# Other weights for prompt attention in the background clock of a one-core decoder step

## The chip, the cores and the metric

One core of one Trainium2 chip runs the whole program in one launch. The metric is the device time of an execution in microseconds (us). The kernel before takes 4103.84 us, the median of three runs (4091.96 to 4107.23). The profiled execution took 4089.54 us, and its trace spans 4087.7 us.

## What is computed

One layer of a decoder for a prompt of 1024 tokens and 64 sample tokens (8 sequences of 8), all in float32. Cut to what matters here:

```
h  = rmsnorm(x) * (1 + scale1) + shift1
z  = h @ w_in                                   # q, k, v, conv inputs, two gates
B  = dilated window attention, 3 head groups, (window, dilation) = (128,1), (512,4), (2048,16)
A  = gated short convolution of z
x += gate1 * ((sigmoid(ga) * (B @ w_attn_o) + sigmoid(gc) * (A @ w_conv_o)) @ w_o)
h  = rmsnorm(x) * (1 + scale2) + shift2
q  = h @ w_query;  scores against 2 x 128 sub-keys; per token and head the best 16 of 16384 experts
x += gate2 * sum over 8 heads x 16 experts of softmax(score) * gelu(h . expert_u[e]) * expert_v[e]
y  = rmsnorm(x)
```

The retrieval reads, for every token, head and choice, one row of `expert_u` and one of `expert_v` (4 KB each).

## The kernel before

The 1088 tokens are nine tiles of up to 128 rows: tiles 0 to 7 are the prompt, tile 8 the sample. The kernel is one function, `peer`, with a program per engine and semaphores between them. Two kinds of work run side by side.

**Jobs.** A job is one head of one tile, 72 in all, of 16 *expert rows* (8 in tile 8). An expert row is the k-th choice of all 128 tokens: GpSimd (POOL) gathers 128 rows of `expert_u` into a ring of 9 slots (L863) and 128 rows of `expert_v` into a ring of 8 (L873), alternately; VectorE (DVE) takes the dot products (L2033); then the weighted sum over `expert_v` is made either by TensorE (PE; `weigh`, L1251, two matmuls of 512 columns by a diagonal matrix) or by DVE (L2049). In jobs 0 to 55 each takes every other row. A gather into a ring slot waits until the row that was there has been used, so POOL waits for PE's `weigh` and for DVE.

**The background.** The dense work is cut in four segments of tiles, (0), (1, 2), (3, 4, 5), (6, 7, 8). For each, `chain_order` lists items in a fixed order: the projection to q, k, v (`qkv`, L1036), the convolution's projections (`conv`, L1143), prompt attention (`s`, `t`, `o`, `oturn`), in the last segment the sample's attention (`kt`, `ss`, `pt`, `so`, `st`), `mix` (L1164), `out` (L1193), and the queries and scores of the jobs (`project`, `turn_q`, `score`, L1220 to L1237). Segment 0 runs ahead of the jobs; the dense work of segment g + 1 runs among the jobs of segment g. Each item goes PE, then ScalarE (ACT) or DVE, through one of four PSUM banks in turn; SyncE (SP) loads weight blocks into a ring of three slots as the items that read the old block finish.

In prompt attention an item is one head of one tile. `s` fills one bank with the scores of up to four blocks of 128 keys (a mask matmul L1074 and a score matmul L1075), DVE takes the row maximum (L1832, L1838), ACT the exponential (L1492), PE transposes the probabilities (`t`, L1111), ACT copies them (L1511), PE multiplies by the values (`o`, L1098) and ACT scales the result (L1521). The scores of the next item are issued before the outputs of this one.

**The clock.** PE, ACT and DVE each run their own list of background items, and after each piece of a job they advance it with `pace.up_to(limit(s, f))`: job s, fraction f done. DVE does so after every expert row, PE after every row that it weighs (three of its own rows ahead), ACT twice a job. `limit` works by the running sum `spent` of `chain_cost` over the items, between *marks* at jobs 0, 5, 21, 45 and 51: between two marks the items that are due are those whose share of the cost is not over the share of expert rows done. So `chain_cost` decides only how the rows between two marks are spread over the items between the same marks:

```
goal = spent[na] + (spent[nb] - spent[na]) * (now - clock(a)) / (clock(b) - clock(a))
due = max(i for i, c in enumerate(spent) if c <= goal)
return min(last_bg, max(na, due, number["score", item_of(min(s + 3, JOBS - 1))]))
```

The stretches between the marks hold 80, 256, 384 and 96 expert rows. Stretch 1 (jobs 0 to 4) holds the dense work of tiles 1 and 2, stretch 2 (jobs 5 to 20) that of tiles 3 to 5, stretch 3 (jobs 21 to 44) that of tiles 6 to 8, stretch 4 queries alone. From job 51 on there is no background. An item of a prompt tile t reads t + 1 blocks of the widest group, up to five of the second and up to two of the first, four blocks to a bank. So the attention of stretch 1 is 8 items with 16 banks of `s` and 16 of `t`, that of stretch 2 12 items with 40 and 40, that of stretch 3 8 items with 32 and 32; and one `oturn` for two items.

Of the kernel before, what the change touches and what calls it, by code (L numbers as in the profile page):

```python
# [237 lines left out]
def cols(g):  # L238
    return prompts(g) * P + (size(g) - prompts(g)) * NS
# [118 lines left out]
def chain_cost(key):  # L358
    name = key[0]
    if name == "conv":  # L360
        return 8 * max(240, cols(key[1])) / 600
    if name == "mix":
        return KC[key[3]] * max(240, cols(key[1])) / 600
    if name == "out":
        a, b = OUT_COLS[key[3]]
        return 8 * (b - a) / 600
    return {"project": 3.4, "qkv": 5.1, "s": 1.2, "o": 1.5, "t": 0.6, "kt": 0.6, "ss": 3.2, "so": 7.5}.get(name, 0.5)


def weight_blocks():  # L370
# [70 lines left out]
def peer(nc, io):  # L441
    with ExitStack() as ctx:
# [120 lines left out]
        for key in number:  # L563
            cost += chain_cost(key)
            spent.append(cost)
# [1624 lines left out]
```

## Time and profile before

| | us |
|---|---|
| median of three runs | 4103.84 |
| profiled execution | 4089.54 |
| its span | 4087.7 |
| PE busy | 3203.6 |
| DVE busy | 2904.9 |
| POOL busy | 2238.6 |
| ACT busy | 671.2 |

The DMA engines moved 1458.83 MB, a mean of 357 GB/s; 1142.49 MB of it by the queue of the expert gathers. The page of the profile cuts the span in 40 equal slices; the view by windows gives the busy time of each engine, the granted TensorE clock (1.00 is 2.4 GHz, 0.50 is 1.2 GHz; a value between is a mean of both), the mean busy share of the 16 DMA engines and what they moved, for any stretch of time. The DMA share counts the time that packets take, and can be a little over 1. The boundaries of the windows below are the starts of the first matmul of each part of the background on PE.

### The profile page before, as it was taken

Reading aid. Unit: us, or ns where it says so; the run is one execution under the profiler, and the core shown is the slowest. Engines: PE = TensorE matmul, PEld = TensorE weight load, DVE = VectorE, ACT = ScalarE, POOL = GpSimd, SP = SyncE. Lnnn points to the kernel's source line nnn. Section 1 sums busy time; section 2 is a strip of 40 time slices with the busy share of each in tenths; the row PEclk is TensorE's granted clock in tenths of the full one; section 3 lists DMA queues with packets and bytes.
Section 4 is the critical chain, followed back from the end, with each engine's and each line's share of the span. In section 5 each row is a group of like instructions: output and inputs, shape, how many; then the busy total and the mean of one; then the engine's idle time right before and its main releaser. Section 6 shows DMA issues by size and latency. Waiting matters only on the chain.

```text
span 4087.7 us, 35782 instructions
## 1 busy us (share of the span) xinstructions
PE 3203.6 (78%) x10406; PEld 1817.5 (44%) x10406; DVE 2904.9 (71%) x6586; ACT 671.2 (16%) x1872; POOL 2238.6 (55%) x2189
## 2 busy tenths in 40 slices
PE   5987989888889998887888977677877765566566
PEld 2575757654445544554444543334544431122222
DVE  1215645678876687677887777767778888888887
ACT  0012021221012211222101331111111110010111
POOL 0003323555554566565665566545657677777765
PEclk8988979999997899998998888788988877788878
DMA  6989969999997899999999899999999999999998
GB/s 207 274 268 334 316 219 315 368 404 383 389 364 244 289 385 398 377 394 382 391 394 366 307 359 366 359 365 363 400 355 406 407 407 409 409 399 409 409 368 319
DMA packets 670924, 1458.83 MB, mean 357 GB/s; under 512 B 53745, under 2 KB 378737, under 8 KB 670705
## 3 DMA queue, kind: packets, MB, share of 16 engines
q0 software_dynamic: 313648, 1142.49, 72.4%
q1 hardware_dynamic: 316596, 267.84, 21.0%
q10 hardware_dynamic: 40488, 46.22, 3.3%
q8 instruction: 87, 1.43, 0.1%
q14 instruction: 105, 0.86, 0.1%
HBM read 1422.53 MB, written 33.83 MB: 356 GB/s over the span
## 4 chain that ended last, share of the span: by engine, by line
DMA 17%; DVE 9%; POOL 9%; PE 8%; issue 5%; SPq 3%; ACT 1%; ACTq 0%; DVEq 0%; POOLq 0%
DMA peer_vring<-in_expert_v,peer_idx 12%; POOL peer_uring L863 4%; POOL peer_vring L873 4%; PE peer_psA L1251 4%; DVE peer_uring L2033 3%; DMA peer_uring<-in_expert_u,peer_idx 2%; DVE peer_acc L2049 2%; SPq L715 2%; SPq L711 1%; DMA peer_w<-in_w_in 1%; DMA peer_w<-in_w_attn_o 1%; PE peer_psB L1075 1%; PE peer_psB L1098 1%; PE peer_psB L1143 1%; DMA peer_arena<-in_x_prompt 1%
## 5 line engine op out<-in xcount | busy, mean ns | idle before, releaser
L1251 PE MATMUL peer_psA<-peer_vring,peer_diag 128*128 128x512 f32 x2336 | 1321.4, 704 | 527.2 <-DMA peer_vring<-in_expert_v,peer_idx 345.9
L873 POOL DMA_INDIRECT peer_vring<-in_expert_v,peer_idx x1088 | 1115.9, 1026 | 1129.2 <-PE peer_psA L1251 837.1
L2033 DVE CUSTOM_DVE_ANT_0 peer_uring<-peer_uring,peer_psH 128x1024 f32<-128x1024 f32 x1088 | 1320.8, 1214 | 327.3 <-DMA peer_uring<-in_expert_u,peer_idx 322.5
L863 POOL DMA_INDIRECT peer_uring<-in_expert_u,peer_idx x1088 | 1117.0, 1027 | 498.9 <-issue 299.2
L1251 PEld LDWEIGHTS peer_psA<-peer_vring,peer_diag 128*128 128x128 f32 x2336 | 485.6, 222 | 1184.5 <-issue 999.5
L2049 DVE SCALAR_TENSOR_TENSOR peer_acc<-peer_vring,peer_coef,peer_acc 128x1024 f32<-128x1024 f32 x495 | 637.1, 1287 | 89.8 <-DMA peer_vring<-in_expert_v,peer_idx 84.3
L1143 PE MATMUL peer_psB<-peer_hT,peer_w 128*128 128x128 f32 (+3 forms) x1152 | 277.0, 399 | 32.7 <-DMA peer_w<-in_w_in 32.5
L1220 PE MATMUL peer_psB<-peer_w,peer_hT 128*128 128x256 f32 x1152 | 275.8, 395 | 30.0 <-DMA peer_w<-in_w_query 29.3
L1036 PE MATMUL peer_psB<-peer_w,peer_hT 128*128 128x384 f32 (+1 forms) x864 | 294.9, 496 | 1.4 <-issue 0.7
L1164 PE MATMUL peer_psB<-peer_hT,peer_w 128*128 128x128 f32 (+3 forms) x1024 | 257.8, 407 | 35.0 <-DMA peer_w<-in_w_attn_o 35.0
L1220 PEld LDWEIGHTS peer_psB<-peer_w,peer_hT 128*128 128x128 f32 x1152 | 229.2, 201 | 89.3 <-DMA peer_w<-in_w_query 31.5
L1143 PEld LDWEIGHTS peer_psB<-peer_hT,peer_w 128*128 128x128 f32 x1152 | 199.2, 193 | 116.7 <-DMA peer_w<-in_w_in 36.3
L1164 PEld LDWEIGHTS peer_psB<-peer_hT,peer_w 128*128 128x128 f32 x1024 | 182.7, 198 | 111.6 <-DMA peer_w<-in_w_attn_o 39.5
L1036 PEld LDWEIGHTS peer_psB<-peer_w,peer_hT 128*128 128x128 f32 (+1 forms) x864 | 161.8, 190 | 131.3 <-issue 44.1
L1698 ACT ACTIVATE peer_g<-peer_g 128x16 f32<-128x16 f32 (+1 forms) x72 | 15.5, 215 | 1139.5 <-DVE peer_g L2063 1138.0
L1649 ACT ACTIVATE peer_diag<-peer_ident,peer_coef 128x128 f32<-128x128 f32 x584 | 178.3, 387 | 54.9 <-DVE peer_coef L2073 54.9
L1832 DVE TENSOR_REDUCE peer_mx<-peer_psB 128x1 f32<-128x512 f32 (+2 forms) x92 | 56.1, 626 | 124.0 <-PE peer_psB L1075 123.4
L1193 PE MATMUL peer_psB<-peer_w,peer_mT 128*128 128x384 f32 (+3 forms) x432 | 130.3, 458 | 6.3 <-issue 4.5
L1075 PE MATMUL peer_psB<-peer_w,peer_mT 64*128 64x256 f32 (+3 forms) x272 | 121.6, 532 | 0.0
L1098 PE MATMUL peer_psB<-peer_w,peer_arena 128*128 128x64 f32 x648 | 102.0, 317 | 24.2 <-ACT peer_arena L1511 24.0
L1098 PEld LDWEIGHTS peer_psB<-peer_w,peer_arena 128*128 128x128 f32 x648 | 99.1, 235 | 35.9 <-issue 35.9
L1193 PEld LDWEIGHTS peer_psB<-peer_w,peer_mT 128*128 128x128 f32 (+1 forms) x432 | 80.8, 188 | 59.0 <-issue 19.7
(201 smaller groups left out, 2738.0 us busy)
## 6 DMA issues: line engine op xcount, KB each, us to landing
peer_w<-in_w_in SPq DMA_DIRECT2D x136, 512.0 KB, 9.0
peer_w<-in_w_in SPq DMA_DIRECT2D x24, 1536.0 KB, 17.1
peer_w<-in_w_query SPq DMA_DIRECT2D x32, 1024.0 KB, 17.0
peer_w<-in_w_ada SPq DMA_DIRECT2D x16, 1536.0 KB, 8.0
peer_uring<-in_expert_u,peer_idx POOLq DMA_INDIRECT x1088, 11.4
peer_vring<-in_expert_v,peer_idx POOLq DMA_INDIRECT x1088, 11.2
peer_w<-in_w_conv_o SPq DMA_DIRECT2D x32, 384.0 KB, 10.0
peer_w<-in_w_o SPq DMA_DIRECT2D x8, 1536.0 KB, 22.2
```

What stands on the lines that cost most here:

```text
L863: pool.indirect_dma_start(out=uring[:, r % U, :], out_offset=None, in_=io["expert_u"], in_offset=bass.IndirectOffsetOnAxis(ap=idx[:, s % 4 ...
L873: pool.indirect_dma_start(out=vring[:, r % V, :], out_offset=None, in_=io["expert_v"], in_offset=bass.IndirectOffsetOnAxis(ap=idx[:, s % 4 ...
L1036: last = pe.matmul(dst[0:R, 0:WQKV], hT[:, k, i * P:i * P + R], wv[:, k, :], start=(k == 0), stop=(k == DC - 1))
L1098: last = pe.matmul(bank(key_o)[:, 0:HD], pT[:, t_slot[g, it, b] % 2, (at % 4) * P:(at % 4 + 1) * P], vv[:, kb, col:col + HD], start=(at == ...
L1143: last = pe.matmul(dst[:, 0:m], wv[:, k, part, :], hT[:, k, 0:m], start=(k == 0), stop=(k == DC - 1))
L1164: last = pe.matmul(dst[:, 0:m], wv[:, KC_AT[q] + k, :], src[:, k, 0:m], start=(k == 0), stop=(k == KC[q] - 1))
L1193: last = pe.matmul(dst[0:R, 0:e - a], mT[:, k, i * P:i * P + R], wv[:, k, :], start=(k == 0), stop=(k == DC - 1))
L1220: last = pe.matmul(dst[:, 0:KD], hT[:, k, j * P:(j + 1) * P], wv[:, k, :], start=(k == 0), stop=(k == DC - 1))
L1251: last = pe.matmul(psA[:, c * 512:(c + 1) * 512], diag[:, a % DG, :], vring[:, r % V, c * 512:(c + 1) * 512], start=first, stop=False, ski ...
L1649: act.activation(diag[:, a % DG, :], ident[:], ACT.Copy, scale=coef[:, s % 4, k:k + 1]).then_inc(diag_set, 1)
L2033: dve.tensor_tensor_reduce(uring[:, r % U, :], uring[:, r % U, :], psH[:], 1.0, 0.0, ALU.mult, ALU.add, act_[:, k:k + 1]).then_inc(u_used, 1)
L2049: dve.scalar_tensor_tensor(out=acc[:], in0=vring[:, r % V, :], scalar=c, in1=acc[:], op0=ALU.mult, op1=ALU.add).then_inc(v_added, 1)
```

## The change

One line of `chain_cost`: an `s` item counts 2.4 in place of 1.2, `o` 4.2 in place of 1.5, `t` 1.0 in place of 0.6. Nothing is computed otherwise, and no instruction is added or removed; the same lists run in the same order on each engine, and the points at which the two kinds of work alternate move.

```diff
@@ def chain_cost(key):
     if name == "out":
         a, b = OUT_COLS[key[3]]
         return 8 * (b - a) / 600
-    return {"project": 3.4, "qkv": 5.1, "s": 1.2, "o": 1.5, "t": 0.6, "kt": 0.6, "ss": 3.2, "so": 7.5}.get(name, 0.5)
+    return {"project": 3.4, "qkv": 5.1, "s": 2.4, "o": 4.2, "t": 1.0, "kt": 0.6, "ss": 3.2, "so": 7.5}.get(name, 0.5)
```

## Rows read from the trace of the kernel before

**Rows 1.** The page: span; DMA tenths and GB/s in 40 slices; bytes.
```profile
span 4087.7 us, 35782 instructions
...
DMA  6989969999997899999999899999999999999998
GB/s 207 274 268 334 316 219 315 368 404 383 389 364 244 289 385 398 377 394 382 391 394 366 307 359 366 359 365 363 400 355 406 407 407 409 409 399 409 409 368 319
DMA packets 670924, 1458.83 MB, mean 357 GB/s; under 512 B 53745, under 2 KB 378737, under 8 KB 670705
```

**Rows 2.** Windows by part of the background: qkv, conv, attention, mix, query; stretch 1.
```profile
core 0: us, PE busy (x) PEld busy (x) DVE busy (x) ACT busy (x) POOL busy (x), PEclk, DMA share, GB/s
359.00:429.80 70.80, 70.80 (x225) 41.67 (x226) 47.79 (x124) 10.84 (x26) 20.03 (x21) 0.96 0.93 335
429.80:504.00 74.20, 74.20 (x318) 59.95 (x316) 43.67 (x103) 5.25 (x17) 32.49 (x32) 1.00 0.97 333
504.00:600.70 96.70, 78.75 (x290) 47.91 (x288) 48.90 (x126) 25.43 (x78) 28.90 (x30) 0.75 0.62 199
600.70:702.90 102.20, 98.67 (x422) 79.79 (x422) 51.75 (x119) 13.21 (x31) 34.75 (x35) 1.00 0.92 310
...
748.30:851.40 103.10, 99.46 (x424) 74.15 (x425) 73.37 (x157) 32.71 (x84) 63.07 (x61) 0.96 1.04 398
```

**Rows 3.** The same view, stretch 2: qkv, conv, attention, mix, out.
```profile
879.30:1037.90 158.60, 144.06 (x421) 78.37 (x420) 132.32 (x298) 22.14 (x56) 91.00 (x90) 0.94 1.03 391
1037.90:1180.80 142.90, 128.53 (x365) 69.65 (x364) 115.05 (x251) 9.10 (x31) 90.15 (x87) 0.95 1.05 386
1180.80:1396.40 215.60, 186.44 (x691) 107.80 (x690) 144.86 (x342) 62.84 (x184) 92.63 (x93) 0.78 0.74 263
1396.40:1591.00 194.60, 181.06 (x506) 97.09 (x504) 150.43 (x325) 35.00 (x76) 128.43 (x122) 0.96 1.04 386
1591.00:1677.40 86.40, 66.11 (x201) 39.05 (x201) 65.89 (x137) 13.08 (x27) 43.50 (x44) 0.93 0.98 375
```

**Rows 4.** The same view, stretch 3: qkv, prompt attention, sample attention, mix.
```profile
1885.60:2070.00 184.40, 157.07 (x442) 75.75 (x441) 153.79 (x345) 23.12 (x64) 120.76 (x113) 0.93 1.00 384
...
2214.00:2380.00 166.00, 137.13 (x557) 77.40 (x556) 128.71 (x296) 55.79 (x155) 88.32 (x87) 0.87 0.93 327
2380.00:2729.20 349.20, 241.24 (x765) 122.68 (x765) 254.12 (x549) 62.26 (x216) 201.55 (x196) 0.81 1.04 364
2729.20:2931.50 202.30, 171.02 (x508) 101.70 (x508) 146.56 (x322) 34.13 (x75) 126.62 (x120) 0.91 1.02 373
```

**Rows 5.** The same view of a stretch without background.
```profile
3400.00:3500.00 100.00, 54.98 (x77) 17.53 (x76) 89.01 (x196) 8.86 (x33) 76.83 (x77) 0.75 1.03 409
```

**Rows 6.** Groups of instructions: transposed probability blocks in the three attention windows.
```profile
L1111 PE MATMUL peer_psB<-peer_ident,peer_arena 128*128 128x128 f32 x56 | 10.0, 325 | 8.0 <-ACT peer_arena L1492 8.0
...
L1111 PE MATMUL peer_psB<-peer_ident,peer_arena 128*128 128x128 f32 x140 | 29.4, 344 | 19.1 <-ACT peer_arena L1492 19.0
...
L1111 PE MATMUL peer_psB<-peer_ident,peer_arena 128*128 128x128 f32 x116 | 21.0, 315 | 7.3 <-ACT peer_arena L1492 7.1
```

**Rows 7.** Waits of POOL in the attention windows of stretches 1 and 2.
```profile
POOL peer_vring L873 <- PE peer_psA L1251: 74.4, 6, 18.7
...
POOL peer_vring L873 <- PE peer_psA L1251: 99.3, 15, 25.6
```

**Rows 8.** Windows, line 1251 alone (PE, PEld): attention 1, mix 1, qkv 2, attention 2, attention 3.
```profile
504.00:600.70 96.70, 21.67 (x32) 7.99 (x32) 0.75 0.62 199
600.70:702.90 102.20, 16.62 (x36) 6.84 (x36) 1.00 0.92 310
...
879.30:1037.90 158.60, 48.04 (x97) 18.36 (x96) 0.94 1.03 391
...
1180.80:1396.40 215.60, 57.42 (x96) 20.40 (x96) 0.78 0.74 263
...
2214.00:2380.00 166.00, 49.33 (x84) 18.28 (x84) 0.87 0.93 327
```

## The prediction

> **What bounds the kernel now.** I read the slices of the page first, then windows cut at the parts of the background, then who waited for whom inside the attention windows. In the slices the reader should look at the DMA digits and the GB/s under them: nearly all slices after the start stand at 9, and the exceptions after slice 5 are slices 6 and 13 to 14 (219, 244 and 289 GB/s), with a shallower one at slice 23 (307) [rows 1]. The windows show what runs there. The 56, 140 and 116 transposed probability blocks are all the blocks of the prompt attention of stretches 1, 2 and 3 (for stretch 2: four heads, 10 + 12 + 13 blocks), so these windows hold that attention and nothing else of the background [rows 6]. In stretch 1 the DMA share is 0.62 in attention against 0.92 to 0.97 around it [rows 2]; in stretch 2 0.74 against 1.03 to 1.05 [rows 3]; in stretch 3 0.93 against 1.00 to 1.04 [rows 4]. Where there is no background, the gathers alone hold 1.03 and 409 GB/s [rows 5]. So outside prompt attention the transfers set the pace from stretch 2 on (in stretch 1 PE does, busy 96 to 100% of qkv, conv and mix [rows 2]), and in prompt attention PE does: 186.4 of 215.6 us in stretch 2, at a granted clock of 0.78, that is partly at 1.2 GHz [rows 3]. The waits say how one starves the other: POOL stood 74.4 us of the 96.7 and 99.3 us of the 215.6 before a gather of `expert_v`, for PE's weighing of the row that held the slot [rows 7]. PE weighs late because its order gives it many attention items between two rows.
>
> **How much the clock moves.** By the code, attention counts 16 x 1.2 + 16 x 0.6 + 8 x 1.5 + 4 x 0.5 = 42.8 in stretch 1, and 90.0 with the new weights; 93.0 and 189.4 in stretch 2 (40 banks, 12 items); 71.6 and 144.4 in stretch 3 (32 banks, 8 items). The sums of the stretches go from 309.1 to 356.3, from 523.2 to 619.6 and from 674.8 to 747.6. The share of attention in the rows of its stretch goes from 80 x 42.8 / 309.1 = 11.1 to 20.2; from 256 x 93.0 / 523.2 = 45.5 to 78.3; from 384 x 71.6 / 674.8 = 40.7 to 74.2. Two gathers make a row, so the trace has 15, 46.5 and 43.5 rows there [rows 2 to 4]: the plan is roughly what happens. So 9.1, 32.8 and 33.5 rows move into attention, out of the other parts of the same stretch in proportion: in stretch 2 from qkv 7.5, conv 7.0, mix 9.3, out 3.3, queries 5.4. No instruction is added, the lists keep their order on every engine, and POOL's order of gathers stays. SP is not paced: its loads follow the freeing of slots, so in the other parts the same weight bytes are asked for in less time, beside fewer gathers. Segment 0, stretch 4 and the jobs after it have no attention or none that is paced, and I put them at zero.
>
> **The price of a row.** On the transfers: 100 us by 38.5 rows is 2.6 us [rows 5]. On PE: 48.0 us by 45 rows in qkv 2 is 1.07, 16.6 by 17.5 in mix 1 is 0.95; in attention, at the lower clock, 21.7 by 15 is 1.44, 57.4 by 46.5 is 1.23, 49.3 by 43.5 is 1.13 [rows 2 to 4, 8]. So a row taken out is worth about 1.0 us where PE sets the pace and 2.6 us where the transfers do. A row put into attention costs nothing on the transfers while they have idle time, 2.6 us after that; on PE 1.1 to 1.4 us, less what it fills of PE's waits.
>
> **Stretch 2.** Out of qkv 7.5 x 2.6 = 19.5 us, if PE lets it: PE's 144.1 less 7.5 x 1.07 is 136.0, and at the 97% that PE reached in mix 1 that takes 140.3 of the 158.6, a gain of 18. Conv by the same steps 18 (128.5 - 7.5 = 121.0 us of PE), mix 17 (181.1 - 8.8 = 172.3, with 0.95 a row), out 8 (PE is idle there for 20 us), the queries 5 to 10 (the first of them, with 99.5 of 103.1 us on PE [rows 2], at PE's price). That is about 68 us. Both PE and DMA would then be within some 3% of full at once, so I take 60, with 54 and 70 as the ends. Into attention: the idle transfers are (1.04 - 0.74) / 1.04 x 215.6 = 62 us, or 24 rows for nothing; the other 8.8 rows take 23 us. PE: 186.4 + 32.8 x 1.23 = 226.8 us, which at 95% busy needs 239 us. Both ways about 240 us, +25. The ends are +5 (PE's clock rises to that of stretch 3, 0.87, where there are more rows to an item [rows 4], and its background part of 129 us shrinks with it) and +46 (PE keeps its present 86% of the window). Net gain 35, from 8 to 65.
>
> **Stretch 3.** All other parts stand at 1.00 to 1.04 of the DMA engines with PE at 69 to 85% [rows 4], so 33.5 rows out give 87 us. Into attention: (1.04 - 0.93) / 1.04 x 166 = 17.6 us are idle, the rest is paid at 2.6: +69.5. PE needs 137.1 + 33.5 x 1.13 = 175 us of the 235 and isn't in the way. Net gain 18, from 10 (qkv stands at 1.00, so part of its rows are worth less) to 18.
>
> **Stretch 1.** PE sets the pace all through. Out: 9.1 x 0.95 = 8.6 us. In: 9.1 x 1.44 = 13 us on PE, of which its idle 18 us [rows 2] can take all or none: 0 to +13. I take +5, since the wait that makes the idle time is PE's for the exponential (8.0 us at the transposes [rows 6]), which a weighed row in between covers. Net gain 4, from -4 to +9.
>
> **A ceiling that would speak against it.** The core moves 1458.83 MB at a mean of 357 GB/s over its span [rows 1]; 409 GB/s are held where only gathers run [rows 5], against 263 GB/s in the attention of stretch 2 [rows 3], so there is room to fill. The Trainium skill, page "DMA: Bandwidth & Descriptors", section "Where 436 GB/s comes from", says that for transfers from HBM into SBUF the HBM share of one core, about 358 GB/s, is what binds. By it the kernel would already stand at its ceiling and the gain would be nothing; the trace disagrees, since it shows 409 GB/s over 100 us.
>
> **The sum.** 35 + 18 + 4 = 57 us off the profiled execution of 4089.5 us is 4032.5 us. That execution lies 14.3 us below the median of the runs, so on the median it is 4103.8 - 57 = 4047 us. The ends give 8 + 10 - 4 = 14 to 65 + 18 + 9 = 92 us, that is 4012 to 4090.
>
> **Rivals.**
> *PE sets the price of both sides.* If PE is as full as its present share in attention allows, rows leave stretch 2 at 1.07 and enter at 1.23: 35 us off and 40 on; stretch 1 gives 8.6 and takes 13; stretch 3 keeps 10 of its 18. Together no change, 4103 us. For it: PE is at 90 to 93% in qkv, conv and mix of stretch 2. Against it: those parts run at 1.03 to 1.05 of the DMA engines, and DVE, POOL and PE all show idle time there, so the transfers come last.
> *The rows get into the attention chain.* From score to maximum to exponential to transposition each step is queued on DVE and ACT behind the row's own work, and with more rows to an item an item could last longer by all of DVE's work for them: 144.9 us by 46.5 rows is 3.1 us a row in stretch 2, 3.0 in stretch 3, 3.3 in stretch 1 [rows 2 to 4]. That gives +102 - 60, +99 - 87 and +30 - 8.6 us, 75 us slower, 4179 us. It decides from about 1.8 us for an added row in stretch 2 (60 / 32.8). For it: ACT waits for the maximum at each item, and PE then for ACT (19.1 us in stretch 2 [rows 6]). Against it: in stretch 3 an item has 5.4 rows against 3.9 in stretch 2, and PE's wait at its transposes is 0.9 us an item there (7.3 by 8) against 1.6 (19.1 by 12) [rows 6], so more rows go with a shorter wait.
> *A limit on the mean rate.* If the transfers are held by a limit that is felt over longer times than a window, so that the mean of 357 GB/s over the span [rows 1] is what the core gets, rows that fill the gaps slow the parts beside them and nothing is gained: 4104 us. [...] Against it: the eight slices from 31 to 38 stand at 399 to 409 GB/s in a row, over 800 us [rows 1].
> That the planner ignores the weights is ruled out by the row counts above, which follow them.
>
> **How the numbers follow.** I give the forecast 0.79, PE's price 0.12, the chain 0.07, the limit on the mean 0.02. A difference of 0.5% (about 20 us) is what a measurement of this kernel can tell from none. The low end of the forecast (14 us) lies inside that and takes 0.02 of its 0.79; a rare slip of PE's price to the slow side adds 0.01 to slower. So faster 0.77, same 0.15, slower 0.08. The range takes the ends 4012 and 4090, with a few us for the spread of runs: 4005 to 4095; left out are the chain, PE's price and the limit on the mean, 0.21 in all, less what the margin takes in.
>
> **What would show it.** Right: attention windows of 95 to 105, about 240 and about 235 us, with some 20 (stretch 1), 78 and 74 rows in them; DMA share near 1.0 in stretches 2 and 3; POOL's wait for PE's weighing in the attention of stretch 2 well below 99 us; its granted clock above 0.78; qkv, conv and mix of stretch 2 shorter by 15 to 20 us each, with PE at 95% or more; stretch 4 and what follows unchanged in length. Wrong: an attention window of stretch 2 over 280 us with PE idle in it (the chain), or qkv, conv and mix of stretch 2 hardly shorter, with PE at 97% or more and DMA under 1.0 (PE's price).

## The result and the profile after

The changed kernel takes 4041.4 us (median of four runs, 4027.5 to 4044.1) against 4105.5 us for the kernel before in the same comparison: a ratio of 0.9851, 95% interval 0.9834 to 0.9867, that is 55 to 68 us faster. The prediction was 4047 us, from 4005 to 4095. Each ratio below is to the kernel before as it ran in the same comparison. Repeated in a later comparison (run `again` below) the changed kernel's ratio was 0.9841 (0.9825 to 0.9858). The profiled execution took 4040.7 us and its span is 48.8 us shorter than that of before; the rest of the difference of the medians is that the profiled execution of before (4089.5 us) was shorter than each of the four runs of this comparison (4092.0 to 4108.9).

The page of the changed kernel; span, DMA busy tenths and GB/s in 40 slices, bytes:

```profile
span 4038.9 us, 35766 instructions
...
DMA  6989979999999999999999999999999999999998
GB/s 204 280 252 327 306 267 321 355 389 396 380 381 347 362 376 366 376 397 382 401 378 372 348 356 362 361 357 371 375 365 405 404 406 409 405 401 409 408 373 318
DMA packets 670924, 1458.83 MB, mean 361 GB/s; under 512 B 53745, under 2 KB 378737, under 8 KB 670705
```

The same bytes in less time; the holes of [rows 1] are shallower. Slices 6, 13 and 14 went from 219, 244 and 289 GB/s to 267, 347 and 362, slice 23 from 307 to 348, and the slices from 31 to 38 stand where they stood.

Windows of the changed kernel, cut as before at the first matmuls of each part (columns as in [rows 2]): attention 1; qkv, conv, attention, mix and out of stretch 2; qkv, prompt attention, sample attention and mix of stretch 3:

```profile
504.80:597.90 93.10, 77.71 (x290) 46.18 (x288) 65.19 (x158) 25.42 (x78) 35.68 (x37) 0.74 0.78 273
858.30:999.10 140.80, 135.35 (x410) 74.69 (x409) 112.37 (x253) 23.42 (x58) 88.38 (x85) 0.99 1.03 388
999.10:1131.60 132.50, 126.52 (x362) 69.30 (x361) 102.74 (x233) 9.35 (x29) 74.81 (x71) 0.97 1.04 376
1131.60:1372.20 240.60, 202.07 (x745) 111.46 (x754) 210.23 (x488) 69.67 (x208) 160.72 (x156) 0.86 0.96 361
1372.20:1552.50 180.30, 170.66 (x485) 92.95 (x483) 136.95 (x300) 29.74 (x62) 107.59 (x106) 0.98 1.05 384
1552.50:1640.30 87.80, 66.96 (x197) 39.28 (x197) 59.19 (x117) 10.40 (x25) 38.96 (x39) 0.88 0.91 337
1830.40:1990.30 159.90, 149.55 (x425) 73.11 (x426) 134.38 (x301) 21.73 (x59) 101.16 (x96) 0.96 1.02 390
2129.50:2362.60 233.10, 175.98 (x610) 95.21 (x617) 197.86 (x452) 61.93 (x177) 147.58 (x144) 0.79 0.96 352
2362.60:2712.40 349.80, 223.54 (x762) 116.25 (x761) 247.01 (x527) 63.29 (x218) 201.76 (x197) 0.82 1.04 364
2712.40:2889.40 177.00, 154.89 (x480) 95.77 (x480) 124.67 (x272) 27.57 (x60) 97.77 (x92) 0.93 1.00 364
```

They answer to [rows 2 to 4]. Two POOL instructions are a row: attention 2 went from 46.5 to 78 rows in 215.6 to 240.6 us, attention 3 from 43.5 to 72 rows in 166.0 to 233.1 us. Attention 1 took 3.5 rows more (15 to 18.5) and is 3.6 us shorter. Of the parts around attention 2, qkv 2 is shorter by 17.8 us with 2.5 rows fewer, conv 2 by 10.4 and mix 2 by 14.3 with 8 rows fewer each; out 2 is not (+1.4). The stretch of 27.9 us ahead of qkv 2 (851.4 to 879.3 us, where PE turns the normed rows, L1019) had 7.5 rows and is now 10.8 us (847.5 to 858.3) with 2. The granted clock of attention 2 rose from 0.78 to 0.86, that of attention 3 fell from 0.87 to 0.79.

POOL's waits in attention 1 and attention 2 of the changed kernel, which answer to [rows 7], and in attention 3:

```profile
POOL peer_vring L873 <- PE peer_psA L1251: 35.1, 5, 20.5
...
POOL peer_vring L873 <- PE peer_psA L1251: 37.6, 12, 8.1
...
POOL peer_vring L873 <- PE peer_psA L1251: 45.1, 10, 11.6
```

From 74.4 and 99.3 us: the gathers stand half as long or less behind rows that PE has not weighed. In attention 3 they stand as long as before (44.0 us then). And the transposes of attention 2 and 3, with PE's idle time before them, which answer to [rows 6]:

```profile
L1111 PE MATMUL peer_psB<-peer_ident,peer_arena 128*128 128x128 f32 x140 | 26.0, 312 | 26.4 <-ACT peer_arena L1492 26.1
...
L1111 PE MATMUL peer_psB<-peer_ident,peer_arena 128*128 128x128 f32 x116 | 23.4, 345 | 21.1 <-ACT peer_arena L1492 21.1
```

PE waits there for the exponential longer than before (19.1 and 7.3 us then).

By stretch: the windows of the whole stretches 1, 2 and 3 before, then after:

```profile
359.00:851.40 492.40, 456.69 (x1788) 325.34 (x1789) 292.31 (x681) 92.58 (x245) 195.06 (x194) 0.93 0.89 315
851.40:1677.40 826.00, 721.57 (x2221) 399.34 (x2219) 626.37 (x1389) 149.93 (x391) 460.92 (x447) 0.90 0.96 354
1677.40:3033.80 1356.40, 1067.78 (x3531) 608.18 (x3531) 1034.92 (x2293) 253.61 (x714) 800.80 (x769) 0.88 1.02 372
```

```profile
361.20:847.50 486.30, 452.14 (x1781) 323.39 (x1782) 294.07 (x685) 92.47 (x245) 189.15 (x187) 0.93 0.91 320
847.50:1640.30 792.80, 709.18 (x2224) 392.76 (x2231) 625.56 (x1394) 146.24 (x389) 473.74 (x459) 0.93 1.00 372
1640.30:2984.50 1344.20, 1054.03 (x3520) 607.51 (x3527) 1027.92 (x2276) 250.80 (x712) 796.05 (x766) 0.88 1.02 373
```

6.1, 33.2 and 12.2 us: 51.5 us of gain, less 2.2 us that the changed kernel starts stretch 1 later. Two thirds is stretch 2.

### The profile page after: what moved, and what is told of

It is laid out like the page before. It is cut to its first block, busy times and chain, and to the rows that moved or that the text cites. A ratio compares the mean times of both kernels' runs of the same rounds, so it can differ in the third digit from the quotient of the medians.

```text
span 4038.9 us, 35766 instructions
## 1 busy us (share of the span) xinstructions
PE 3164.6 (78%) x10390; PEld 1806.9 (45%) x10406; DVE 2901.7 (72%) x6586; ACT 665.0 (16%) x1867; POOL 2241.4 (55%) x2189
## 4 chain that ended last, share of the span: by engine, by line
DMA 15%; PE 9%; POOL 9%; DVE 8%; SPq 5%; issue 5%; ACT 1%; ACTq 0%; POOLq 0%; DVEq 0%
DMA peer_vring<-in_expert_v,peer_idx 9%; POOL peer_uring L863 5%; POOL peer_vring L873 4%; PE peer_psA L1251 4%; SPq L715 3%; DMA peer_uring<-in_expert_u,peer_idx 2%; DVE peer_uring L2033 2%; DMA peer_w<-keys_turned 1%; DVE peer_acc L2049 1%; PE peer_psB L1143 1%; PE peer_psB L1164 1%; DMA peer_w<-in_w_attn_o 1%; DMA peer_w<-in_w_in 1%; PE peer_psB L1036 1%; SPq L198 1%
## 5 line engine op out<-in xcount | busy, mean ns | idle before, releaser
L1251 PE MATMUL peer_psA<-peer_vring,peer_diag 128*128 128x512 f32 x2336 | 1291.0, 691 | 478.4 <-DMA peer_vring<-in_expert_v,peer_idx 320.4
L1251 PEld LDWEIGHTS peer_psA<-peer_vring,peer_diag 128*128 128x128 f32 x2336 | 475.9, 217 | 1113.6 <-issue 938.3
L1220 PEld LDWEIGHTS peer_psB<-peer_w,peer_hT 128*128 128x128 f32 x1152 | 232.5, 204 | 92.4 <-DMA peer_w<-in_w_query 34.9
L1649 ACT ACTIVATE peer_diag<-peer_ident,peer_coef 128x128 f32<-128x128 f32 x584 | 178.3, 387 | 54.5 <-DVE peer_coef L2073 54.5
L1193 PE MATMUL peer_psB<-peer_w,peer_mT 128*128 128x384 f32 (+3 forms) x432 | 132.1, 463 | 6.2 <-DVE peer_mT L1917 3.7
L1913 DVE TENSOR_TENSOR peer_arena<-peer_arena,peer_psB 128x128 f32<-128x128 f32 (+3 forms) x64 | 27.6, 435 | 143.7 <-PE peer_psB L1164 140.8
L1075 PE MATMUL peer_psB<-peer_w,peer_mT 64*128 64x256 f32 (+3 forms) x272 | 120.5, 527 | 3.0 <-issue 1.1
L1098 PE MATMUL peer_psB<-peer_w,peer_arena 128*128 128x64 f32 x648 | 97.5, 308 | 24.3 <-ACT peer_arena L1511 24.1
L1098 PEld LDWEIGHTS peer_psB<-peer_w,peer_arena 128*128 128x128 f32 x648 | 96.1, 227 | 41.9 <-issue 31.9
## 6 DMA issues: line engine op xcount, KB each, us to landing
peer_w<-in_w_query SPq DMA_DIRECT2D x32, 1024.0 KB, 17.2
```

The lines of the kernel that those rows point to most:

```text
L1098: last = pe.matmul(bank(key_o)[:, 0:HD], pT[:, t_slot[g, it, b] % 2, (at % 4) * P:(at % 4 + 1) * P], vv[:, kb, col:col + HD], start=(at == ...
L1193: last = pe.matmul(dst[0:R, 0:e - a], mT[:, k, i * P:i * P + R], wv[:, k, :], start=(k == 0), stop=(k == DC - 1))
L1220: last = pe.matmul(dst[:, 0:KD], hT[:, k, j * P:(j + 1) * P], wv[:, k, :], start=(k == 0), stop=(k == DC - 1))
L1251: last = pe.matmul(psA[:, c * 512:(c + 1) * 512], diag[:, a % DG, :], vring[:, r % V, c * 512:(c + 1) * 512], start=first, stop=False, ski ...
L1649: act.activation(diag[:, a % DG, :], ident[:], ACT.Copy, scale=coef[:, s % 4, k:k + 1]).then_inc(diag_set, 1)
```

## The experiments

The theory under test: rows moved into prompt attention run in time that POOL, DVE and the transfers had idle, and give time back where they leave, because the transfers are full there. It has these rivals: PE sets the price on both sides; a longer attention chain; a split inside the item, not the number of rows; PE's clock; POOL's own issue in place of the transfers.

**One stretch alone.**

In `chain_cost` of the kernel before, the new weights for one stretch only:

```diff
+    if name in ("s", "o", "t") and key[1] == 2:
+        return {"s": 2.4, "o": 4.2, "t": 1.0}[name]
     return {"project": 3.4, "qkv": 5.1, "s": 1.2, "o": 1.5, "t": 0.6, "kt": 0.6, "ss": 3.2, "so": 7.5}.get(name, 0.5)
```

This is `only2`; `only3` has 3 for the 2.

> The new weights in stretch 2 alone (tiles 3 to 5), the old ones elsewhere. Theory (rows moved into attention fill idle transfers, and are worth 2.6 us where they leave): 33 to 35 us faster than the kernel before, a ratio of about 0.992; the attention window of stretch 2 at about 240 us, stretches 1 and 3 as before. PE's price on both sides: no change, ratio 1.000.

> The new weights in stretch 3 alone (tiles 6 and 7 of the prompt). Theory: the idle transfers of its attention, 10 to 18 us, ratio 0.9955 to 0.9975, although the granted clock there does not rise. If the gain came from PE's clock: nothing in this stretch, ratio 1.000.

`only2`: 4055.4 us, ratio 0.9888 (0.9856 to 0.9921). `only3`: 4093.3 us, ratio 0.9990 (0.9974 to 1.0006). The three stretches, of `only2` and then of `only3`:

```profile
360.00:851.60 491.60, 452.94 (x1780) 323.62 (x1781) 291.71 (x680) 92.47 (x245) 188.18 (x186) 0.93 0.90 315
851.60:1649.70 798.10, 718.32 (x2233) 396.23 (x2231) 626.72 (x1397) 146.27 (x389) 475.22 (x459) 0.92 0.99 370
1649.70:3004.40 1354.70, 1068.86 (x3527) 608.40 (x3527) 1031.83 (x2283) 253.54 (x714) 798.42 (x766) 0.88 1.01 371
```

```profile
851.60:1687.50 835.90, 727.11 (x2221) 403.31 (x2219) 630.48 (x1397) 149.93 (x391) 458.59 (x446) 0.89 0.95 351
1687.50:3037.40 1349.90, 1056.24 (x3531) 608.35 (x3531) 1031.46 (x2287) 250.88 (x712) 796.25 (x769) 0.87 1.02 373
```

Stretch 2 alone carries most of the gain (27.9 us in the profile, 32 to 59 by the interval), and leaves its neighbours where they were. PE's price on both sides, which gave no change, falls. Stretch 3 alone is 6.5 us shorter in the profile and not told from no change in the runs (the interval goes from 2 us slower to 11 faster): under the 10 to 18 us expected. `only3` also shows how far two profiles differ: its stretch 2 has the old weights and is 9.9 us longer than in the kernel before (835.9 and 826.0).

**The same rows, another split inside the item.**

```diff
-    ... "s": 2.4, "o": 4.2, "t": 1.0, ...
+    ... "s": 2.48, "o": 3.1, "t": 1.24, ...
```

> s 2.48, o 3.1, t 1.24: the old weights of attention, all by the same factor, so that attention has nearly the rows of the changed kernel (19.6, 78.1, 74.8 against 20.2, 78.3, 74.2) but another split inside an item. Theory (only the number of rows in attention counts): as the changed kernel, within 0.3%, ratio to before 0.982 to 0.988. If it is the place of the rows inside an item that counts (more of them behind the outputs, where PE waited for the exponential): clearly less gain, ratio over 0.990.

4047.1 us, ratio 0.9878 (0.9843 to 0.9913). The interval holds the changed kernel's 0.9851 and reaches just over 0.990: the number of rows gives most of the gain; whether the split is worth the 0.3% between the two is left open. Stretch 1 gained nothing in its profile (493.5 us, against 492.4 before and 486.3 changed).

**Half of the way, and twice the way.**

```diff
-    ... "s": 2.4, "o": 4.2, "t": 1.0, ...
+    ... "s": 1.8, "o": 2.25, "t": 0.9, ...         # mid
+    ... "s": 4.8, "o": 8.4, "t": 2.0, ...          # fourfold
```

> Half the way: s 1.8, o 2.25, t 0.9, that is the old weights by 1.5; attention has 15, 62 and 58 rows (11, 46 and 41 before, 20, 78 and 74 changed). Theory (the first rows into the attention of stretch 2 are nearly free, since neither POOL, DVE nor the transfers are full there; later ones cost up to 2.6 us): more than half of the gain, 35 to 45 us under the kernel before, with attention 2 at 218 to 228 us. If each row in costs the same: half the gain, some 30 us.

> Attention at twice the new weights (s 4.8, o 8.4, t 2.0): 32, 119 and 124 rows in place of 20, 78 and 74. Theory: the idle transfers are filled already, so the 41 and 49 further rows cost 2.6 us each in attention, and where they leave they give 1.1 us (stretch 2, PE full) and some 1.8 us (stretch 3): +63, +40 and some 3 us, about 4145 us, slower than before by 1%. If more rows in attention simply help: under 4041 us. If each further row lengthened the attention chain by DVE's 3.1 us: about 4180 us.

`mid`: 4071.1 us, ratio 0.9934 (0.9908 to 0.9960), 16 to 38 us of gain, about half. `fourfold`: 4095.2 us, ratio 0.9987 (0.9971 to 1.0002); the gain is gone, but by the ratios it costs some 56 us on the changed kernel, not the 104 expected. Stretch 1, stretch 2 and attention 2 of `mid`:

```profile
358.60:860.00 501.40, 459.78 (x1785) 322.59 (x1786) 290.39 (x676) 92.30 (x245) 189.93 (x190) 0.92 0.88 308
860.00:1657.70 797.70, 705.11 (x2224) 389.42 (x2222) 627.26 (x1395) 147.19 (x390) 460.53 (x452) 0.92 1.00 371
...
1165.20:1387.70 222.50, 188.11 (x723) 104.83 (x722) 182.60 (x426) 66.66 (x197) 128.78 (x127) 0.84 0.91 332
```

Stretch 2 and attention 2 of `fourfold`, where PE's wait for the exponential at the transposes comes to 52.8 us:

```profile
844.30:1676.00 831.70, 710.86 (x2240) 395.72 (x2237) 643.44 (x1437) 144.35 (x387) 481.73 (x465) 0.91 0.98 360
...
1100.10:1445.70 345.60, 245.27 (x828) 130.89 (x827) 308.61 (x697) 79.84 (x235) 247.14 (x234) 0.81 0.99 377
```

| stretch 2 | before | mid | changed | fourfold |
|---|---|---|---|---|
| rows in attention, planned | 45.5 | 62.2 | 78.3 | 119.4 |
| rows in attention, by POOL | 46.5 | 63.5 | 78 | 117 |
| attention, us | 215.6 | 222.5 | 240.6 | 345.6 |
| rows outside attention, by POOL | 177 | 162.5 | 151.5 | 115.5 |
| the rest of the stretch, us | 610.4 | 575.2 | 552.2 | 486.1 |
| whole stretch, us | 826.0 | 797.7 | 792.8 | 831.7 |

The price of a row that enters climbs: 6.9 us for the first 17 rows (0.4 each), 18.1 for the next 14.5 (1.2), 105.0 for the last 39 (2.7). The last step is clear. The one from 0.4 to 1.2 is not: with the same weights attention 2 took 240.6 us in the changed kernel and 247.8 in `only2`. Fewer rows left the rest of the stretch than entered attention, since the stretch as a whole took up to 9 rows more. By the rows that left, each gave 35.2 / 14.5 = 2.4 us, then 23.0 / 11 = 2.1, then 66.1 / 36 = 1.8, not PE's 1.1. So the first half of the rows brought 28.3 of the 33.2 us of this stretch, as the theory had it. As a whole `mid` gained only half, the figure for a row price that does not climb: its stretch 1 is 9.0 us longer than before, most of it in its qkv (77.2 us for 70.8), and no run here shows why.

**Half of the bytes.** Each gather reads 2 KB in place of 4 KB: index e takes the e-th piece of 2 KB, and the other half of each ring slot is set to zero once, ahead of the jobs. So these two kernels leave out the layer's true sum over the experts; the number of gathers and all other work stay.

```diff
+    half_u, half_v = (io[a].rearrange("e (h d) -> (e h) d", h=2) for a in ("expert_u", "expert_v"))
-    out=uring[:, r % U, :], out_offset=None, in_=io["expert_u"],
+    out=uring[:, r % U, 0:D // 2], out_offset=None, in_=half_u,     # vring and half_v likewise
```

> The old weights, and each gather reads 2 KB of a row in place of 4 KB (the other half of each ring slot is zero, so the experts' part of the output is left out of account); all other work and the number of gathers are as before. Theory (outside attention the transfers set the pace): the parts of stretches 2 and 3 then fall to PE's or DVE's time, about 3800 to 3900 us; the stretch without background goes from 2.6 us a row to DVE's 2.3. Rival (POOL's own time to issue a gather, 1.0 us and 0.3 us idle each, 2.6 us a row, sets the pace and the DMA share only shows its effect): 4000 us or more, and still 2.5 to 2.6 us a row.

> The new weights, with the same half gathers. Theory: with transfers to spare everywhere a row leaves the other parts of stretch 2 at PE's 1.1 us, so the change gives less than half of its gain: 0 to 30 us under the half gathers with the old weights. Rival (POOL's issue sets the pace): the gain stays at 50 to 60 us.

`half_before`: 3843.1 us; `half_after`: 3830.1 us, ratios to the kernel before 0.9382 (0.9346 to 0.9418) and 0.9341 (0.9319 to 0.9364). With half the bytes the change is worth some 13 us by the medians, with intervals that overlap, so it isn't told from none; with whole rows it was worth 61. qkv, conv, attention, mix of stretch 2 and attention 3, of `half_before` and then `half_after`:

```profile
857.50:1016.50 159.00, 143.56 (x421) 78.21 (x420) 132.46 (x300) 22.61 (x59) 101.49 (x98) 0.95 0.76 235
1016.50:1142.60 126.10, 125.95 (x366) 68.99 (x365) 113.69 (x254) 9.11 (x31) 93.64 (x87) 1.00 0.83 260
1142.60:1356.60 214.00, 182.61 (x682) 106.49 (x691) 145.34 (x344) 62.96 (x184) 92.96 (x93) 0.78 0.51 143
1356.60:1533.40 176.80, 175.86 (x506) 95.60 (x505) 147.69 (x319) 35.00 (x75) 128.15 (x121) 1.00 0.84 256
2096.10:2262.20 166.10, 136.35 (x550) 77.41 (x556) 128.14 (x296) 55.85 (x155) 89.95 (x87) 0.87 0.63 178
```

```profile
851.00:991.80 140.80, 135.34 (x410) 74.39 (x409) 113.36 (x256) 23.42 (x58) 87.13 (x85) 0.99 0.76 235
991.80:1123.90 132.10, 126.07 (x362) 68.98 (x361) 102.70 (x233) 9.34 (x29) 77.29 (x72) 0.97 0.73 220
1123.90:1351.00 227.10, 197.54 (x745) 110.98 (x754) 212.00 (x494) 69.66 (x208) 161.14 (x156) 0.87 0.72 211
1351.00:1524.50 173.50, 169.36 (x485) 92.78 (x484) 132.78 (x296) 29.74 (x62) 109.02 (x105) 0.98 0.79 240
2050.50:2281.50 231.00, 178.58 (x609) 96.51 (x616) 200.33 (x456) 61.72 (x177) 151.18 (x144) 0.78 0.67 194
```

The whole stretches 2 and 3 of `half_before`, and then of `half_after`:

```profile
840.80:1610.20 769.40, 703.59 (x2212) 394.12 (x2219) 618.70 (x1386) 150.07 (x391) 466.81 (x446) 0.92 0.72 220
1610.20:2793.30 1183.10, 1022.73 (x3523) 592.28 (x3530) 1013.52 (x2280) 252.88 (x714) 806.94 (x770) 0.92 0.84 254
```

```profile
840.20:1608.60 768.40, 700.88 (x2224) 390.47 (x2231) 630.46 (x1419) 146.22 (x389) 479.45 (x459) 0.94 0.74 226
1608.60:2790.80 1182.20, 1026.06 (x3520) 596.64 (x3527) 1009.53 (x2272) 250.41 (x712) 804.95 (x766) 0.91 0.84 254
```

What the change takes and gives in each profile, in us (the rest of a stretch is its length less its attention):

| | attention | rest | sum |
|---|---|---|---|
| stretch 2, whole rows | +25.0 | -58.2 | -33.2 |
| stretch 2, half rows | +13.1 | -14.1 | -1.0 |
| stretch 3, whole rows | +67.1 | -79.3 | -12.2 |
| stretch 3, half rows | +64.9 | -65.8 | -0.9 |

So in stretch 2 the gain does need transfers that set the pace where the rows leave: with the old weights conv 2 (142.9 to 126.1 us) and mix 2 (194.6 to 176.8) are at once at PE's time with half the bytes, and then moving rows out of them gives nothing or next to nothing (126.1 to 132.1 and 176.8 to 173.5). In stretch 3 it is not so simple: the rows that leave still give 65.8 of the 79.3 us with half the bytes, 2.2 us each by POOL's count, and no run here shows what they are paid in. Attention 3 isn't paid in transfers: it takes 166 us with the old weights and 231 to 233 with the new, whatever the bytes. Attention 2 with the new weights is, in part: 240.6 us fall to 227.1. And qkv 2 isn't held by the transfers at all: 158.6 and 159.0 us with the old weights, 140.8 and 140.8 with the new. Of its 17.8 us, 10.2 are one wait of PE before a weighing (it ends at 988.7 us of the kernel before, just after ACT, which was closing a tile at L1655, has made the diagonal matrix at L1649); `half_before` has the same wait; the changed kernel and `half_after` don't.

The rival of POOL's issue is right for the part of the kernel without background. POOL's instructions there, 3400 to 3700 us of the kernel before and 3150 to 3450 us of `half_before`:

```profile
L873 POOL DMA_INDIRECT peer_vring<-in_expert_v,peer_idx x114 | 115.1, 1010 | 36.5 <-issue 31.4 <-PE peer_psA L1251 5.1
L863 POOL DMA_INDIRECT peer_uring<-in_expert_u,peer_idx x113 | 115.1, 1019 | 34.4 <-issue 30.8 <-DVE peer_act L2033 3.7
```

```profile
L865 POOL DMA_INDIRECT peer_uring<-in_expert_u,peer_idx x112 | 125.9, 1124 | 34.1 <-issue 23.8 <-DVE peer_act L2035 10.4
L875 POOL DMA_INDIRECT peer_vring<-in_expert_v,peer_idx x111 | 107.1, 964 | 33.8 <-issue 28.6 <-DVE peer_acc L2051 3.0 <-PE peer_psA L1253 2.1
```

227 and 223 gathers in 300 us: 2.6 and 2.7 us a row, at 406 and 201 GB/s. POOL is busy or between two instructions for 292 of the 300 us before, and a row takes no less time when the bytes are halved. At 4 KB the transfers are near full as well: from issue to landing a gather took 11.3 us there (median), and 3.8 us with half the bytes.

**More rows into another part that isn't full.** In the changed kernel:

```diff
-        return 8 * (b - a) / 600
+        return 12 * (b - a) / 600          # chain_cost of "out"
```

> The new weights of attention, and out items at 12 in place of 8: out has 9, 26 and 33 rows in place of 7, 18 and 23. Theory (rows into a part whose engines and transfers are not full are cheap; out 2 stands at 0.91 of the transfers and PE at 79%): 5 to 12 us faster than the changed kernel. If out ends as late as its rows make it (2.6 us a row): no change or up to 10 us slower.

> The changed kernel once more, as the standard for the others on the same chip: ratio to before 0.983 to 0.987.

`again` (the changed kernel): 4036.5 us, ratio 0.9841 (0.9825 to 0.9858). `out15`: 4074.2 us, ratio 0.9927 (0.9911 to 0.9943): 38 us slower than the changed kernel, a miss of both expectations. qkv 2, out 2 and out 3 of `out15`, then out 2 and out 3 of `again`, whose qkv 2 is 140.8 us with 85 gathers, as in the changed kernel above:

```profile
853.10:1001.40 148.30, 138.13 (x409) 75.76 (x408) 109.71 (x248) 21.45 (x55) 80.97 (x81) 0.97 1.00 372
1561.00:1657.00 96.00, 70.32 (x208) 40.90 (x208) 80.20 (x166) 13.08 (x27) 54.04 (x51) 0.88 1.01 393
2894.40:3016.60 122.20, 83.94 (x226) 43.04 (x226) 95.58 (x199) 17.16 (x42) 63.58 (x63) 0.82 1.01 381
```

```profile
1544.50:1631.40 86.90, 65.13 (x198) 38.19 (x197) 58.49 (x116) 10.40 (x25) 40.49 (x40) 0.89 0.91 341
2877.60:2973.20 95.60, 70.52 (x211) 37.56 (x211) 74.18 (x153) 14.20 (x31) 45.90 (x46) 0.90 1.01 379
```

Out 2 took 5.5 more rows for 9.1 us and out 3 8.5 for 26.6 us, 1.7 and 3.1 us a row. Out 3 was full to begin with (1.01), which the expectation left out. But qkv 2 became 7.5 us longer with two rows fewer, and attention 3 12.6 us longer (245.1 against 232.5) with 4 rows more, while sample attention gave 17.1 us for 12.5 rows. Where the rows fall inside a part may matter as well as how many they are; the sums here don't cover that, and no run isolates it.

**Off DVE, onto PE.** In the changed kernel:

```diff
-    return k in ((1, 3, 5, 7, 9, 11, 13, 15) if s < WINDOW else (2, 5, 8, 11, 14))
+    return k in ((1, 3, 5, 7, 9, 11, 13, 15) if s < WINDOW and not 29 <= s < 34 else (2, 5, 8, 11, 14))
```

> The new weights; in jobs 29 to 33, those of the prompt attention of stretch 3, DVE adds 5 of 16 rows and PE weighs 11, in place of 8 and 8. Takes 15 additions of 1.29 us from DVE (19 us) and gives PE 15 rows of 2.8 us (four records of 0.705 us: 42 us). If DVE sets the pace of that window: 233 falls to about 215 us. If PE does: up to 250 us or more. If POOL or the transfers do: no change.

4048.6 us, ratio 0.9863 (0.9844 to 0.9881): 12 us above `again`, with intervals that overlap. Attention 3 of `dve5`, then of `again`:

```profile
2131.70:2369.50 237.80, 196.02 (x673) 101.22 (x672) 185.74 (x443) 66.52 (x193) 152.92 (x149) 0.85 0.95 351
```

```profile
2123.50:2356.00 232.50, 178.80 (x618) 96.05 (x617) 197.81 (x453) 61.82 (x177) 148.92 (x144) 0.79 0.96 352
```

DVE has 12.1 us less, PE 17.2 more, the window is 5.3 us longer. DVE alone doesn't set that window, and PE's work goes mostly into its idle time; since one gets what the other loses, the run doesn't test either by itself. With the half rows, which leave it at 231 us, the transfers are out too. POOL is no likelier: in attention 3 of the changed kernel it stood 45.1 us for PE's weighing, and 39.7 in `half_after`. What is left is the chain from PE to DVE to ACT and back, which no run isolates.

## Why the prediction was right, and where its steps were not

The sum gave 57 us; the profile has 48.8, the medians 64.

- *Which stretch and which part.* Right: attention of stretches 1 and 2 starved the gathers, the waits of POOL on PE fell by half and more, and stretch 2 gave 33.2 us (35 predicted, 8 to 65). Stretch 1 gave 6.1 (4, from -4 to 9), but not by its step: 3.5 rows moved, not 9.1, attention got 3.6 us shorter where it should have got 5 longer, and `scaled`, with nearly the same rows planned, has no gain there. That figure was luck.
- *How many rows move.* Right for stretch 2 (31.5 against 32.8 planned). In stretch 3 28.5 against 33.5, since the attention of before already had 43.5, not 40.7, and sample attention kept all of its rows (98 and 98.5 by POOL) and its 349 us, where the plan took 9.5 rows from it, 25 us at 2.6; why it kept them is not shown.
- *The length of attention.* 240 and 235 us predicted, 240.6 and 233.1 measured; 93.1 in stretch 1, outside the 95 to 105. For attention 3 the length was right and the reason was not, which is luck: the step paid all but 17.6 us of the entry at 2.6 us a row on the transfers, and half the bytes leave attention 3 as long as it was. In attention 2 half the bytes took the entry from 25.0 to 13.1 us, so there about half of it was paid in transfers. What sets the price in attention 3 is not settled; POOL's waits and `dve5` leave the chain.
- *Rows leave at the transfers' price.* Right in kind for conv 2 and mix 2, which the transfers held, but with 8 rows fewer each they gave 10.4 and 14.3 us, 1.3 and 1.8 a row, against 18 and 17 forecast: they reached PE's time. Failed for qkv 2, which is as long with half the bytes and gave 17.8 us for 2.5 rows, not 7.5; for out 2, which gave nothing in place of 8 us; and for the queries, of which the first (743.1 to 847.5 us) takes 104.4 us for 103.1 with 4 rows fewer. The stretch's first 27.9 us, the turning of the normed rows, gave 17.1 us for 5.5 rows and has no term in the sum. So that the rest came to 58.2 us against 60 is in part luck: its terms were exchanged.
- *Stretch 3.* Mis-sized: 12.2 us, and 6.5 alone, against 18 (10 to 18). The step counted all 17.6 us of idle transfers in its attention as won. They are not: its attention stands at 0.96 now, (1.04 - 0.96) / 1.04 x 233.1 = 18 us idle as before. The gain there came from the rest, which gave 79.3 us for the 30 rows that left it, 2.6 each as in the sum. Attention took 67.1 us for 28.5 rows, which at 2.6 would be 74.1: so the idle time was worth 7 us, not 17.6.
- *PE in attention.* The clock of attention 2 rose as said, to 0.86, and PE's busy time grew by 15.6 us where 40 were counted for the rows. Part of that is the clock: the same instructions of L1075, L1098 and L1111 took 127.8 us of PE before and 115.1 after. But the higher clock doesn't give the gain by itself: with half the bytes it rises in the same way (0.78 to 0.87) and the stretch gains 1.0 us, and in attention 3 `dve5` has it at 0.85 for 0.79 without being shorter.
- *The chain.* Its decision point was 1.8 us a row in stretch 2; the price is 0.8 on average there (25.0 / 31.5). But it exists: PE's wait for the exponential grew from 19.1 to 26.4 us and to 52.8 in `fourfold`, and in stretch 3 the argument against it (more rows go with a shorter wait) was not borne out, 7.3 us became 21.1. It didn't hold in the rows of before either: there PE waited another 8.5 us for the same exponential at the mask matmul (L1074), against 0.7 in stretch 2.
- *The limit on the mean rate.* The mean rose from 357 to 361 GB/s, and the gain came; this rival falls. The Trainium skill, page "DMA: Bandwidth & Descriptors", section "Where 436 GB/s comes from", puts the limit for transfers from HBM into SBUF at about 358 GB/s. The trace disagrees: slices 31 to 38 of the changed kernel stand at 401 to 409 GB/s.

## What to carry to other kernels

When two streams of work share the engines by a clock of estimated costs, read the estimate against the slices in which the transfers fall: an item whose cost is too low crowds out the other stream, and there the first units moved in are the cheap ones (0.4 to 1.2 us a row here, then 2.7), while each gives back 2.4 to 1.8 us where it leaves. Move until the entry price reaches the exit price and stop: a like step into the out items, of which those of stretch 3 were already full, cost 38 us. To learn what a share of transfers near 1.0 means, halve the bytes and see which parts get shorter: here conv 2 and mix 2 did, qkv 2 and the gathers by themselves did not.

## What was not expected of the hardware

A part that shows a DMA share of 1.02 and 406 GB/s need not get faster with fewer bytes: with 2 KB gathered in place of 4 KB the share fell to 0.70 and 201 GB/s, and a row still took 2.7 us. In these two stretches an indirect gather of 128 rows held POOL for 1.0 us (means of 0.96 to 1.12), with 0.3 us before the next, at either size. So POOL's issue and the transfers happened to meet at 4 KB a row; whether a faster issue would help at 4 KB no run here shows.
